# Two layers, two modulations: the second one's products and sums issued from the convolution's projection

## The chip, the core and the metric

The kernel is one program on one NeuronCore of a Trainium2 chip. TensorE multiplies matrices into PSUM (eight banks of 128 x 512 fp32), VectorE, ScalarE and GpSimd work beside it, and SyncE issues most of the loads. The engines run in parallel, each through its own list of instructions in order, and meet at semaphores. The metric is the time of one execution on the device, in microseconds, as the median of several runs.

## What is computed

A first block of two residual layers (sparse attention, then an RWKV mixer, each followed by a squared-ReLU feed-forward layer) and a second block of two conditioned layers (a short convolution, then dilated attention) on 256 tokens of 1024 features, all in fp32. What matters here is the conditioning of the second block:

```python
def adaln_pre_norm(x, c, g, w_mod, b_mod):
    mod = jax.nn.silu(c) @ w_mod + b_mod
    shift, scale, gate = jnp.split(mod, 3, axis=-1)
    h = rms_norm_2(x, g, NORM_EPS) * (1.0 + scale[:, None, :]) + shift[:, None, :]
    return h, gate

def short_conv_mixer(h, w_in, conv_k, w_out):
    b_gate, c_gate, xin, z = jnp.split(h @ w_in, 4, axis=-1)
    t = c_gate * xin
    ...
    return (b_gate * conv * jax.nn.silu(z)) @ w_out

# second block, i = 0 (convolution) and 1 (dilated attention)
    h, gate = adaln_pre_norm(x, c, norm_g[i], w_mod[i], b_mod[i])
    ...
    x = x + gate[:, None, :] * y
```

The modulation (shift, scale and gate) of both layers depends only on the condition `c` and the weights, so it can be worked out at any time before its use. That of layer 0 is used by the convolution, that of layer 1 by the dilated attention.

## The kernel before

The stages run one after the other: `dsa`, `mlp(0)`, `rwkv_in`, `rwkv_mid`, `scan_loop`, `rwkv_out`, `mlp(1)`, `mid_norm` (the first block's final norm, VectorE only), `conv`, `dilated`, `final_norm`. Each engine has a function of each of these names.

**Granules.** All large weights come in granules of 128 x 1024 fp32 (512 KB) through a ring of four slots (`RING = 4`). SyncE loads granule g into `raw`, ScalarE rounds it to `w_hi` (L585), VectorE takes the remainder `w_lo` (L1064), and TensorE multiplies it three times (hi by hi, lo by hi, hi by lo). ScalarE may round granule g once TensorE is done with granule g - 4. A block of the convolution's projection (`feature_granule`, L1765 to L1767) is four granules, 24 products each, into two banks. There are four blocks in each of two halves of the features: xin into banks 0 and 1, the gate c into 2 and 3, the gate b into 4 and 5, z into 6 and 7.

**Modulation.** During `mlp(l)` GpSimd loads the 24 pieces of `w_mod[l]` (L486), ScalarE scales them by the condition (L754) and GpSimd adds them up into `mod_all` (L492, L494). At the end of `mlp(l)`, after the last down product (L1950 to L1952), TensorE's `modulation(l)` sums `mod_all` over the partitions: 16 products of one column each give shift and scale in bank 7 (L1974), and two products of 512 columns give the gate in banks 6 and 0 (L1978). As fp32 each is two records in the profile, so 32 and 4. TensorE then waits until VectorE has taken them (`mod_ready`, four counts a layer): VectorE adds the bias (L1300), makes the gain (L1302) and adds both halves of the gate (L1307).

**The way into the convolution.** VectorE adds the down products to X (L1293), takes one more remainder (L1064), does its `modulation(1)`, and scales X in `mid_norm` (L1603) when GpSimd has the roots of the mean squares (L470, L472), which ScalarE's squares (L603) of the unscaled X feed. Then come the squares of the scaled X, their roots, the normalised rows (`normalise`, L1074), TensorE's transposes into banks 4 to 7 (L1789), gain and shift on VectorE (L1085), the rounding on ScalarE (L614), the remainder on VectorE (L1096) and the first product of the projection.

Of the kernel before, what the change touches and what calls it, by code (L numbers as in the profile page):

```python
# [8 lines left out]
F32R = mybir.dt.float32r  # L21
# [5 lines left out]
P = 128  # L27
SEQ = 256
TILES = SEQ // P
D = 1024  # L30
# [111 lines left out]
def program(nc, A, out):  # L142
    parts, _, parts_bf = shape_constants()
    with ExitStack() as keep:
# [101 lines left out]
        def mlp_plan(t):  # L246
            return dict(relu=t("ff_relu", [P, 2, BLOCK]), sq=t("ff_sq", [P, 2, BLOCK]),
                        mod_w=t("mod_w", [P, 3, D]),
                        mod_all=t("mod_all", [P, 3 * D]),
                        hi=t("ff_hi", [P, 2, 4, SEQ], F32R), lo=t("ff_lo", [P, 2, 4, SEQ], F32R))  # L250

# [807 lines left out]
        def _(dve):  # L1059
# [185 lines left out]
            def mlp(l, following):  # L1245
# [48 lines left out]
                split_lo(STREAM[following], PER_BLOCK - 1)  # L1294
                modulation(l)

            def modulation(l):

                dve.wait_ge(mod_full, 3 * l + 1)
                dve.tensor_tensor(mod_col[:, l, :], bank[7][:, 0:2 * KT], B_MOD[l], ALU.add).then_inc(mod_ready, 1)  # L1300
                dve.wait_ge(mod_ready, 4 * l + 1)
                dve.scalar_tensor_tensor(gain[:, l, :], mod_col[:, l, KT:2 * KT], 1.0, NORM2[l], ALU.add, ALU.mult).then_inc(mod_ready, 1)  # L1302
                dve.wait_ge(gate_loaded, 32)
                for n, b in enumerate((6, 0)):
                    dve.wait_ge(mod_full, 3 * l + 2 + n)
                    to = gate[:, l, n * BLOCK:(n + 1) * BLOCK]
                    dve.tensor_tensor(to, to, bank[b][:, :], ALU.add).then_inc(mod_ready, 1)  # L1307
# [297 lines left out]
            def conv():  # L1605
                base = STREAM["conv"]
                dve.wait_ge(x_updated, 18)
                normalise(5)
                dve.wait_ge(mod_ready, 8)
                scale_and_split(5, 4, gain[:, 0, :], mod_col[:, 0, 0:KT])  # L1610
# [8 lines left out]
                for half in range(2):  # L1619
                    at = 16 * half  # L1620
                    split_block(base, at + 4)
                    split_block(base, at + 8)

# [36 lines left out]
            def dilated():  # L1660
                base = STREAM["dil"]
                normalise(6)
                scale_and_split(6, 6, gain[:, 1, :], mod_col[:, 1, 0:KT])

# [73 lines left out]
        def _(pe):  # L1738
# [190 lines left out]
            def mlp(l):  # L1929
# [35 lines left out]
                down(FF_STEPS - 1, 4, 1, False, True)  # L1965
                modulation(l)

            def modulation(l):

                for n in range(3):  # L1970
                    pe.wait_ge(mod_used[n], KT * (l + 1))
                pe.wait_ge(up_relu, 2 * FF_STEPS * (l + 1))
                for k in range(2 * KT):
                    mm = pe.matmul(bank[7][:, k:k + 1], M["mod_all"][:, k * P:(k + 1) * P], ones[:, 0:1], start=True, stop=True)  # L1974
                mm.then_inc(mod_full, 1)
                for n, b in enumerate((6, 0)):
                    at = 2 * D + n * BLOCK
                    pe.matmul(bank[b][:, :], ones, M["mod_all"][:, at:at + BLOCK], start=True, stop=True).then_inc(mod_full, 1)  # L1978
                pe.wait_ge(mod_ready, 4 * (l + 1))

# [285 lines left out]
            def conv():  # L2266
# [3 lines left out]
                for half in range(2):  # L2270

                    for n, (left, count) in enumerate(((conv_x, 1), (conv_t, 1), (conv_b, 1), (conv_z, 2))):
                        if half:
                            pe.wait_ge(left, count)
                        for q in range(PER_BLOCK):
                            if n == half == 0:
                                wait_act(4, q)
                            g = base + 16 * half + 4 * n + q
                            feature_granule(g, g % RING, hi, lo, q, (bank[2 * n], bank[2 * n + 1]))
                pe.wait_ge(conv_x, 2)  # L2280
                pe.wait_ge(conv_t, 2)
# [106 lines left out]
```

## Time and profile before

| | us |
|---|---|
| median of 3 runs | 1340.64 |
| the runs | 1334.78 to 1341.19 |
| span of the profiled execution | 1330.5 |
| TensorE busy in it | 1210.7 |
| VectorE busy | 875.3 |
| ScalarE busy | 675.9 |
| GpSimd busy | 185.7 |

The span runs from the first to the last instruction; the runs' times also hold what lies around it. Times in rows are us from the span's start. The mean granted TensorE clock of the profiled execution is 0.954 of full speed. PE is TensorE, PEld its weight loads, DVE is VectorE, ACT ScalarE, POOL GpSimd. A row of a timeline gives the start, the time that its instructions cover, their line, what is written and read, how many there are, and in brackets how long the engine had no work before and who ended that.

### The profile page before, as it was taken

What the parts mean: (1) busy time and instruction counts of PE and PEld (TensorE: products, weight loads), DVE (VectorE), ACT (ScalarE), POOL (GpSimd) and SP (SyncE); (2) the same over time, 40 slices, a digit from 0 to 9 for tenths busy, and PEclk for the clock granted to TensorE, in tenths of its full rate; (3) what the DMA queues carried; (4) which work ended last, traced back from release to release, by engine and by line L of the source; (5) the groups of instructions that cost most, each with busy time, mean ns of one, the idle gap of its engine ahead of it and who ended that gap; (6) DMA issues with size and microseconds to landing.
All of it is one profiled execution on the core that took longest, in us unless ns stands there. A gap on an engine that the chain in (4) does not pass through costs nothing.

```text
span 1330.5 us, 21999 instructions
## 1 busy us (share of the span) xinstructions
PE 1210.7 (91%) x8300; PEld 1076.5 (81%) x8304; DVE 875.3 (66%) x1238; ACT 675.9 (51%) x1006; POOL 185.7 (14%) x168
## 2 busy tenths in 40 slices
PE   6889899999699789898989899998899799999986
PEld 5777798997598468887967889896899699998775
DVE  4785558687776566656436667777576777775674
ACT  4764465656254723333344556564443456665552
POOL 1000124345200010000000225253000000000000
PEclk9989999999899979899998999999899899999999
DMA  7321567876545100000003677776355645566300
GB/s 277 126 81 47 179 233 251 265 244 230 167 143 174 63 1 1 0 0 20 0 1 95 210 251 249 263 251 197 114 188 165 185 132 185 188 189 195 123 1 32
DMA packets 81882, 190.12 MB, mean 143 GB/s; under 512 B 5841, under 2 KB 6113, under 8 KB 81697
## 3 DMA queue, kind: packets, MB, share of 16 engines
q1 hardware_dynamic: 72896, 157.31, 36.5%
q0 software_dynamic: 7632, 27.59, 7.0%
q10 hardware_dynamic: 1296, 4.44, 0.9%
q8 instruction: 38, 0.62, 0.2%
q14 instruction: 20, 0.16, 0.0%
HBM read 188.27 MB, written 1.05 MB: 142 GB/s over the span
## 4 chain that ended last, share of the span: by engine, by line
PE 79%; DVE 10%; ACT 3%; issue 3%; POOL 2%; DMA 2%; ACTq 0%; DVEq 0%; POOLq 0%; SPq 0%
PE bank L1765 12%; PE bank L1767 12%; PE bank L1766 12%; PE bank L2080 7%; PE bank L1748 4%; PE bank L1750 4%; PE bank L1749 4%; PE bank L1950 4%; PE bank L1952 4%; PE bank L1951 4%; PE bank L2172 1%; POOL mod_all L494 1%; PE bank L1789 1%; PE bank L1991 1%; PE bank L2045 1%
## 5 line engine op out<-in xcount | busy, mean ns | idle before, releaser
L1064 DVE TENSOR_TENSOR w_lo<-raw,w_hi 128x1024 fp32r<-128x1024 f32 x296 | 390.8, 1336 | 248.6 <-ACT w_hi L585 248.5
L585 ACT ACTIVATE w_hi<-raw 128x1024 fp32r<-128x1024 f32 x296 | 311.8, 1058 | 348.5 <-PE bank L1767 176.7
L1765 PE MATMUL bank<-act_hi,w_hi 128*128 128x256 f32 x1392 | 391.9, 282 | 15.0 <-DMA rows_of<-in_rows_of_dram 9.4
L1767 PE MATMUL bank<-act_hi,w_lo 128*128 128x256 f32 x1392 | 390.8, 281 | 0.0
L1766 PE MATMUL bank<-act_lo,w_hi 128*128 128x256 f32 x1392 | 390.7, 281 | 0.0
L1765 PEld LDWEIGHTS bank<-act_hi,w_hi 128*128 128x128 f32 x1392 | 262.9, 189 | 17.3 <-DMA rows_of<-in_rows_of_dram 9.7
L1766 PEld LDWEIGHTS bank<-act_lo,w_hi 128*128 128x128 f32 x1392 | 262.9, 189 | 0.7 <-issue 0.2
L1767 PEld LDWEIGHTS bank<-act_hi,w_lo 128*128 128x128 f32 x1392 | 262.8, 189 | 0.0
L494 POOL TENSOR_TENSOR mod_all<-mod_all,mod_w 128x1024 f32<-128x1024 f32 x42 | 110.0, 2618 | 143.0 <-ACT mod_w L754 142.1
L1950 PE MATMUL bank<-w_hi,ff_hi 128*128 128x512 f32 x256 | 103.4, 404 | 5.9 <-DVE ff_lo L1262 5.9
L470 POOL TENSOR_SCALAR stat<-stat 128x1 f32<-128x1 f32 x16 | 9.0, 560 | 678.7 <-ACT xn L603 678.4
L1952 PE MATMUL bank<-w_hi,ff_lo 128*128 128x512 f32 x256 | 102.3, 400 | 0.0
L1951 PE MATMUL bank<-w_lo,ff_hi 128*128 128x512 f32 x256 | 101.6, 397 | 0.0
L1748 PE MATMUL bank<-w_hi,act_hi 128*128 128x512 f32 x224 | 89.8, 401 | 1.6 <-DVE act_lo L1585 1.2
L1750 PE MATMUL bank<-w_hi,act_lo 128*128 128x512 f32 x224 | 89.5, 400 | 0.0
L1749 PE MATMUL bank<-w_lo,act_hi 128*128 128x512 f32 x224 | 89.1, 398 | 0.0
L886 ACT ACTIVATE v_inv<-bank 128x512 f32<-128x512 f32 x56 | 33.4, 596 | 60.0 <-PE bank L2085 27.8
L1950 PEld LDWEIGHTS bank<-w_hi,ff_hi 128*128 128x128 f32 x256 | 48.9, 191 | 17.4 <-DVE w_lo L1064 6.7
L1952 PEld LDWEIGHTS bank<-w_hi,ff_lo 128*128 128x128 f32 x256 | 48.7, 190 | 12.6
L1951 PEld LDWEIGHTS bank<-w_lo,ff_hi 128*128 128x128 f32 x256 | 48.9, 191 | 11.1
L754 ACT ACTIVATE mod_w<-mod_w,c_col 128x1024 f32<-128x1024 f32 x48 | 51.7, 1137 | 6.0 <-DMA mod_w<-in_w_mod_dram 6.0
L1748 PEld LDWEIGHTS bank<-w_hi,act_hi 128*128 128x128 f32 x224 | 42.7, 190 | 13.7 <-DVE act_lo L1585 1.9
(285 smaller groups left out, 1734.0 us busy)
## 6 DMA issues: line engine op xcount, KB each, us to landing
raw<-in_mlp_w_up_dram SPq DMA_DIRECT2D x64, 512.0 KB, 4.9
raw<-in_mlp_w_down_dram SPq DMA_DIRECT2D x64, 512.0 KB, 4.3
raw<-in_dil_w_in_dram SPq DMA_DIRECT2D x64, 512.0 KB, 3.9
mod_w<-in_w_mod_dram POOLq DMA_DIRECT2D x48, 512.0 KB, 4.3
raw<-in_conv_w_in_dram SPq DMA_DIRECT2D x32, 512.0 KB, 3.6
raw<-in_rwkv_w_rkv_dram SPq DMA_DIRECT2D x24, 512.0 KB, 4.6
raw<-in_dsa_w_in_dram SPq DMA_DIRECT2D x16, 512.0 KB, 5.2
raw<-in_dsa_w_o_dram SPq DMA_DIRECT2D x8, 512.0 KB, 3.6
```

The source lines that it names most:

```text
L494: pool.tensor_tensor(total, total, part, ALU.add).then_inc(mod_used[n], 1)
L585: act.activation(w_hi[:, slot, :], raw[:, slot, :], ACT.Copy).then_inc(hi_ready, 1)
L1064: dve.tensor_tensor(w_lo[:, slot, :], raw[:, slot, :], w_hi[:, slot, :].bitcast(F32), ALU.subtract).then_inc(lo_ready, 1)
L1748: pe.matmul(dst, x_hi, w_hi[:, slot, at], start=begin, stop=False, skip_group_check=True)
L1749: pe.matmul(dst, x_hi, w_lo[:, slot, at], start=False, stop=False, skip_group_check=True)
L1750: mm = pe.matmul(dst, x_lo, w_hi[:, slot, at], start=False, stop=end, skip_group_check=True)
L1765: pe.matmul(dst, w_hi[:, slot, at], hi[:, kt, :], start=begin, stop=False, skip_group_check=True)
L1766: pe.matmul(dst, w_hi[:, slot, at], lo[:, kt, :], start=False, stop=False, skip_group_check=True)
L1767: mm = pe.matmul(dst, w_lo[:, slot, at], hi[:, kt, :], start=False, stop=end, skip_group_check=True)
L1950: pe.matmul(dst, x_hi, w_hi[:, at_slot, at], start=first and q == 0, stop=False, skip_group_check=True)
L1951: pe.matmul(dst, x_hi, w_lo[:, at_slot, at], start=False, stop=False, skip_group_check=True)
L1952: mm = pe.matmul(dst, x_lo, w_hi[:, at_slot, at], start=False, stop=last and q == PER_BLOCK - 1, skip_group_check=True)
```

## The change

The modulation of layer 1 is no longer issued at the end of `mlp(1)`, by neither TensorE nor VectorE; that of layer 0 stays at the end of `mlp(0)`.

- TensorE issues it in `conv`, after the first of the eight blocks of the projection. Its gate products go to banks 6 and 4, as bank 0 then holds the projection's xin.
- VectorE takes it in `conv` after the remainders of granules 4 to 7.
- TensorE waits for VectorE's part (`mod_ready`, 8) ahead of the third block, which writes bank 4, and no longer at the end of `mlp(1)`; for layer 0 that wait now stands in `mlp`.
- VectorE's wait for `mod_ready` in the convolution is for 4 instead of 8, and the dilated layer has one for 8.
- `mod_all` moves behind `ff_hi` and `ff_lo` in SBUF, so that the convolution's tiles don't lie over it.

```diff
         def mlp_plan(t):
             return dict(relu=t("ff_relu", [P, 2, BLOCK]), sq=t("ff_sq", [P, 2, BLOCK]),
                         mod_w=t("mod_w", [P, 3, D]),
-                        mod_all=t("mod_all", [P, 3 * D]),
-                        hi=t("ff_hi", [P, 2, 4, SEQ], F32R), lo=t("ff_lo", [P, 2, 4, SEQ], F32R))
+                        hi=t("ff_hi", [P, 2, 4, SEQ], F32R), lo=t("ff_lo", [P, 2, 4, SEQ], F32R),
+                        mod_all=t("mod_all", [P, 3 * D]))
...
                 split_lo(STREAM[following], PER_BLOCK - 1)
-                modulation(l)
+                if l == 0:
+                    modulation(l)
...
-                for n, b in enumerate((6, 0)):
+                for n, b in enumerate((6, 4 * l)):
                     dve.wait_ge(mod_full, 3 * l + 2 + n)
...
                 normalise(5)
-                dve.wait_ge(mod_ready, 8)
+                dve.wait_ge(mod_ready, 4)
                 scale_and_split(5, 4, gain[:, 0, :], mod_col[:, 0, 0:KT])
...
                     split_block(base, at + 4)
+                    if half == 0:
+                        modulation(1)
                     split_block(base, at + 8)
...
                 normalise(6)
+                dve.wait_ge(mod_ready, 8)
                 scale_and_split(6, 6, gain[:, 1, :], mod_col[:, 1, 0:KT])
...
                 down(FF_STEPS - 1, 4, 1, False, True)
-                modulation(l)
+                if l == 0:
+                    modulation(l)
+                    pe.wait_ge(mod_ready, 4)
...
-                for n, b in enumerate((6, 0)):
+                for n, b in enumerate((6, 4 * l)):
                     at = 2 * D + n * BLOCK
                     pe.matmul(bank[b][:, :], ones, M["mod_all"][:, at:at + BLOCK], start=True, stop=True).then_inc(mod_full, 1)
-                pe.wait_ge(mod_ready, 4 * (l + 1))
...
                         if half:
                             pe.wait_ge(left, count)
+                        elif n == 2:
+                            pe.wait_ge(mod_ready, 8)
                         for q in range(PER_BLOCK):
                             if n == half == 0:
                                 wait_act(4, q)
                             g = base + 16 * half + 4 * n + q
                             feature_granule(g, g % RING, hi, lo, q, (bank[2 * n], bank[2 * n + 1]))
+                        if n == half == 0:
+                            modulation(1)
```

## Rows read from the trace of the kernel before

**Rows 1.** The page: the chain by engine, and the costliest matmul group.
```profile
PE 79%; DVE 10%; ACT 3%; issue 3%; POOL 2%; DMA 2%; ACTq 0%; DVEq 0%; POOLq 0%; SPq 0%
...
L1765 PE MATMUL bank<-act_hi,w_hi 128*128 128x256 f32 x1392 | 391.9, 282 | 15.0 <-DMA rows_of<-in_rows_of_dram 9.4
```

**Rows 2.** Chain of waits, 924 to 941: start, duration, work or "issue".
```profile
924.63 3.46 PE bank L1974 x32
928.09 2.52 PE bank L1978 x4
...
934.07 0.56 POOL stat L472
...
934.73 0.76 DVE xn L1074
...
940.66 0.38 PE bank L1765
```

**Rows 3.** Timeline of VectorE, 921 to 945: start, duration, instruction, [idle before, releaser].
```profile
927.06 1.22 DVE L1064 TENSOR_TENSOR w_lo<-raw,w_hi 128x1024 fp32r<-128x1024 f32 x1
...
930.64 0.69 DVE L1307 TENSOR_TENSOR gate<-gate,bank 128x512 f32<-128x512 f32 x1 [0.79 <-PE bank L1978]
931.25 2.47 DVE L1603 SCALAR_TENSOR_TENSOR X<-X,stat,scale_row 128x1024 f32<-128x1024 f32 x2
```

**Rows 4.** Stretches by time: length; busy PE, PEld, DVE, ACT, POOL; TensorE clock; DMA.
```profile
912.10:915.30 3.20, 3.20 (x10) 2.42 (x9) 3.20 (x3) 1.15 (x2) 0.00 (x0) 0.50 0.76 224
924.60:928.80 4.20, 4.20 (x35) 3.82 (x34) 3.87 (x7) 3.36 (x5) 1.42 (x2) 1.00 0.43 126
929.50:939.00 9.50, 4.48 (x18) 3.28 (x16) 5.83 (x8) 2.30 (x4) 2.32 (x7) 0.50 0.32 107
941.00:1052.00 111.00, 111.00 (x859) 106.89 (x858) 70.74 (x90) 50.06 (x54) 0.00 (x0) 1.00 0.57 176
```

**Rows 5.** Waits: TensorE's (941 to 1052), then all engines' (951.9 to 1030).
```profile
PE bank L1765 <- DVE act_lo L1096: 1.4, 1, 1.4
...
ACT w_hi L585 <- PE bank L1767: 43.5, 26, 1.8
DVE w_lo L1064 <- ACT w_hi L585: 28.5, 21, 1.9
```

**Rows 6.** Timeline of TensorE at the transposes in front of the convolution.
```profile
935.63 3.01 PE L1789 MATMUL bank<-const,xn 128*128 128x128 f32 x13 [5.02 <-DVE xn L1074]
```

**Rows 7.** Timeline of GpSimd, 900 to 985.
```profile
927.30 1.03 POOL L470 TENSOR_SCALAR stat<-stat 128x1 f32<-128x1 f32 x1 [18.11 <-ACT xn L603]
928.41 0.58 POOL L472 TENSOR_TENSOR stat<-stat,half_neg 128x1 f32<-128x1 f32 x1
929.08 0.19 POOL L470 TENSOR_SCALAR stat<-stat 128x1 f32<-128x1 f32 x1
929.35 0.55 POOL L472 TENSOR_TENSOR stat<-stat,half_neg 128x1 f32<-128x1 f32 x1
```

**Rows 8.** Timeline of TensorE at the first layer's modulation, 343 to 351.
```profile
343.38 3.63 PE L1974 MATMUL bank<-const,mod_all 128*128 128x1 f32 x32
346.86 1.96 PE L1978 MATMUL bank<-mod_all,const 128*128 128x512 f32 x4
```

**Rows 9.** Stretches by time around the first layer's modulation, columns as in group 4.
```profile
362.10:365.50 3.40, 3.40 (x17) 3.40 (x18) 1.64 (x4) 0.63 (x1) 0.00 (x0) 0.50 0.00 0
366.30:369.70 3.40, 3.40 (x31) 3.40 (x30) 1.22 (x1) 1.07 (x2) 0.00 (x0) 1.00 0.00 0
343.40:350.20 6.80, 5.42 (x37) 4.12 (x35) 5.89 (x11) 3.36 (x5) 2.88 (x6) 1.00 0.49 162
```

**Rows 10.** Timeline of VectorE, 945 to 1090: the remainder of granule 7.
```profile
953.38 1.23 DVE L1064 TENSOR_TENSOR w_lo<-raw,w_hi 128x1024 fp32r<-128x1024 f32 x1 [1.59 <-ACT w_hi L585]
```

**Rows 11.** Stretches by time at the dilated layer's start, columns as in group 4.
```profile
1058.90:1062.00 3.10, 3.10 (x15) 3.10 (x16) 1.43 (x3) 0.00 (x0) 0.55 (x1) 0.50 0.47 153
1064.10:1067.50 3.40, 3.40 (x29) 3.40 (x30) 3.30 (x7) 1.55 (x3) 0.00 (x0) 1.00 0.00 0
```

## The prediction, made before the changed kernel was run

> **What bounds the kernel now.** I read the page first: TensorE stands for 79% of the chain that ended last, VectorE for 10% [rows 1]. So nearly everything waits for TensorE, but only averaged over stages; the change touches two, and each is read by itself.
>
> The first is the end of the second feed-forward layer. Its last product gives way at 924.63, and the chain of waits shows what follows until the convolution's first product at 940.66 [rows 2]: 3.46 us of one-column modulation products, 2.52 us of gate products, the last gate addition, the scaling of X from 931.25, its square on ScalarE, the root on GpSimd, the normalisation, the transposes, the modulated rows and their rounding. VectorE's timeline gives the same stretch from the other side [rows 3]: a weight remainder at 927.06, and at 930.64 the last gate addition after 0.79 us without work, ended by L1978. That addition stands straight in front of L1603.
>
> The second is the convolution's projection. The stretches by time show TensorE busy for all of 941 to 1052, at full clock [rows 4]. The lists of waits (951.9 to 1030) put ScalarE behind TensorE (43.5 us in 26 waits) and VectorE behind ScalarE (28.5 us in 21), and have no wait of TensorE in it [rows 5]. TensorE is the bound there and the others are paced by the ring of four granules.
>
> The change therefore takes TensorE work out of a place where TensorE then idles for 5.02 us [rows 6] and puts it into a place where it never idles.
>
> **Removed at the end of the feed-forward layer.** What is late next, once the modulation is gone? L1603 for the first row tile needs three things. VectorE is free of L1293 and its last w_lo at 927.06 + 1.22 = 928.28 [rows 3]. The bank sums in X are there. The root of the first tile ends on GpSimd at 928.41 + 0.58 = 928.99 [rows 7]. The root is the last, and L1074 starts 0.10 us after such a root (934.07 + 0.56 = 934.63, start 934.73) [rows 2]. So L1603 starts at 929.09 in place of 931.25: 2.16 us earlier. All that follows it up to 940.66 hangs on it in a chain [rows 2] and moves with it. Of the 5.98 us of TensorE work that leave, only these 2.16 us come back, as the path under them ran on VectorE, ScalarE and GpSimd anyway. Bounds: VectorE now runs L1603 while GpSimd works out the root of the second tile. L470 took 1.03 us beside a busy VectorE and 0.19 us alone [rows 7]; at the worst that root ends at 929.90 + 0.84 = 930.74, and the second L1603, due at 929.09 + 1.24 = 930.33, starts 0.5 us late. Gain 1.6 to 2.16 us; I take 2.16 because the second tile is ready at 929.90 if nothing interferes. The gate products also ran slower here (the clock was 1.00 up to 928.8 and 0.50 from 929.5 [rows 4]; 2.52 us against 1.96 us in the first layer [rows 2, 8]). Where it doesn't fall there, 0.6 us less is removed: lower bound 1.0 us.
>
> **Added to the projection.** After the first block (four granules, 96 products) TensorE runs the same 32 one-column records and four 512-column records. At full clock, in the first layer, they start at 343.38 and 346.86, so the first group takes 3.48 us; the second is busy for 1.96 us [rows 8], of which the next product would overlap about 0.17 us (a 256-column product lasts 0.28 us and they start 3.4/31 = 0.11 us apart [rows 1, 9]). Added: 3.48 + 1.96 - 0.17 = 5.27 us. TensorE idles nowhere in the projection, so all of it is on the path. Bounds 5.1 us (twice the overlap) and 5.98 us (3.46 + 2.52, half clock included [rows 2]).
>
> Does a later stall absorb it? In all of 941 to 1052 TensorE waits once, the 1.4 us in front of the first product [rows 5]. So nothing is given back, and the two terms sum to 5.27 - 2.16 = +3.11 us.
>
> **The moved waits.** VectorE takes its modulation after the remainders of granules 4 to 7 (the last of them starts at 953.38 and takes 1.23 us [rows 10], so it ends at 952.45 after the shift) and stands in front of granule 8. By the sum the first block (96 products at 3.4/29 = 0.117 us [rows 11], 11.2 us from 940.66 on) ends at 951.9 - 2.16 = 949.8, the last gate product at 955.0 and the last gate addition (0.69 us [rows 3]) ends at about 955.9. Granule 8's slot is free only when granule 4 is used, 2.8 us into the second block, at 957.9, and ScalarE's rounding comes first. Queued behind VectorE's wait are therefore only remainders that cannot start yet: cost nothing, margin over 2 us, and TensorE itself needs granule 8 only at 966. TensorE's new wait for the eighth modulation count stands at the third block, 11 us after the gate products: nothing. The removed wait at the end of the layer was over at 930.64 + 0.69 = 931.33 [rows 3], while TensorE waited for xn until 935.63 [rows 6]: nothing. VectorE's wait for count 4 in the convolution and for count 8 in the dilated layer have long been met: nothing. DMAs: none is moved. The weights' modulated sums are complete on GpSimd before 927.30 - 18.11 = 909.19, where its idle stretch begins [rows 7], and GpSimd's queue isn't passed by anything. The new place of mod_all only keeps the convolution's tiles off it.
>
> **The clock.** Two questions, both read from the granted clock. First, the products of the projection's start. TensorE will now stand idle from 924.6 to about 933.5 and then transpose. Before, the clock was 0.50 (1.2 GHz) from 929.5 to 939, transposes included, and 1.00 (2.4 GHz) from 941 [rows 4]. At the dilated layer's start the same happened: 0.50 under its transposes at 1058.9 to 1062, 1.00 from 1064.1 under its first products [rows 11]. In both, the projection behind the transposes ran at full clock, so I cost this at nothing.
>
> The Trainium skill (TensorE: Matmul & The Clock Gate, Part 4) says that in transpose mode the full clock isn't reached, as such work doesn't count as busy. By that rule the first products of the projection would run at half clock, as in the rival "cold start" below. The trace speaks against it in both places: 1.00 under the projection, after transposes that began at 0.50 [rows 4, 11].
>
> Second, the one-column products in mid-stream. In this layer they were followed by a fall to 0.50 between 928.8 and 929.5, with TensorE busy all the time from 924.6 [rows 2, 4]. In the first layer the clock was 1.00 over the products and after them (343.4 to 350.2) [rows 9]. So it can go either way. I take a fall, as the longer dense stretch behind them makes it dear and one of two shows it. A short slow stretch lasts from 912.1 to 915.3 [rows 4]. Its price comes from the products after 362: 17 in 3.4 us at half clock, 31 in 3.4 us at full clock [rows 9], that is 14 too few at 3.4/31 = 0.11 us, or 1.5 us (both counts take in products cut by the edges). Bounds: nothing, and two such stretches, 3.1 us.
>
> **Sum.** -2.16 + 5.27 + 1.5 = +4.6 us on the profiled execution, 1330.5 to 1335.1 us of span. The median of the runs, 1340.64, lies 10.1 us above that span, the lowest run, 1334.78, 4.3 us; I add the difference to the median: 1345.2 us, or +0.34%.
>
> **The rivals.**
> - *No fall of the clock in the projection* (speaks for it: the first layer): +3.11 us, 1343.8. Chance 0.22.
> - *Cold start*, by the longer idle stretch or because transposes don't raise the clock: they leave the clock at half and the projection's first 3.4 us run slow, on top of the fall behind the modulation: 3.11 + 1.5 + 1.5 = +6.1, 1346.8. Against it: the two places above. Chance 0.10. The Trainium skill's rule would end here.
> - *Slower by more than can be missed*: the one-column products hold the clock down over two stretches. This is one mechanism, from 950 on in the projection, where weight loads fill TensorE but each product is one column. It is 3.11 + 3.1 = +6.2 with the gain at its full size, and with the gain at its lower bound of 1.0 us +7.4, 1348.0. It decides against the kernel from two slow stretches on. Chance 0.18.
> - *The moved products cost nothing*, as TensorE isn't what paces the projection: -2.16, 1338.5. For it: ScalarE and VectorE each work only half of the time and could catch up. Against: they wait for TensorE, not it for them [rows 5]. Chance 0.05.
> - *The removal gives nothing*, as GpSimd's roots are as late as the gate was: 5.27 + 1.5 = +6.8, 1347.4. Against: 928.99 and 929.90 [rows 7]. Chance 0.03.
> - The forecast has the rest, 0.42.
>
> **How the numbers follow.** About 0.5% (6.7 us) is what a measurement of this kernel can tell from no change; the three runs shown already differ by 6.4 us. Faster by more than that (below 1333.9) comes out of no case but the spread of the runs: 0.03. Slower by more (above 1347.3) takes the slower rival, half of the removal that gives nothing, and a part of cold start: 0.20. The rest is 0.77. The range goes from the case in which the products are free (1338.5), a little lower for the spread of the runs, to the slower rival: 1337.5 to 1349.
>
> **What the profile after should show.** L1603 starts about 4.5 us after the last down product (6.6 us before). TensorE idles about 9 us in front of its transposes, in place of 5.0. The 36 modulation records stand between the convolution's first and second block with no idle time before or behind them and take 5.3 us. From the last down product to the end of the convolution's last block the time grows by 3 to 5 us, and behind that everything is shifted alike. If VectorE's w_lo for granule 8 comes later than 1.5 us after its slot is free, the step on the moved wait is wrong. If the stretch behind the modulation has a clock of 1.00, the clock term is wrong. If TensorE shows an idle stretch in the projection before or after, so is the claim that it is the bound.

## The result: 0.5% slower, and the profile after

The changed kernel took 1344.38 us (median of 10 runs, 1339.68 to 1345.73) against 1337.55 us for the kernel before (10 runs, 1330.52 to 1341.39). The ratio is 1.005 with a 95% interval of 1.0030 to 1.0069: 6.7 us slower, between 4.0 and 9.2. The forecast was +4.6 us, 1345.2 us; it stood on the first three runs of the kernel before, whose median was 3.1 us above that of the ten.

The page of the changed kernel (span, then the chain that ended last by engine):

```profile
span 1341.1 us, 22000 instructions
...
PE 79%; DVE 10%; ACT 3%; issue 3%; POOL 2%; DMA 2%; ACTq 0%; DVEq 0%; POOLq 0%; SPq 0%
```

The shares are those of [rows 1]. The difference is in two stages, so they are read like the stages before. First the end of the feed-forward layer. VectorE's timeline of the changed kernel, against [rows 3]:

```profile
927.24 2.48 DVE L1281 TENSOR_TENSOR X<-X,bank 128x512 f32<-128x512 f32 x4 [0.42 <-PE bank L1944]
929.63 1.22 DVE L1052 TENSOR_TENSOR w_lo<-raw,w_hi 128x1024 fp32r<-128x1024 f32 x1
931.66 1.29 DVE L1592 SCALAR_TENSOR_TENSOR X<-X,stat,scale_row 128x1024 f32<-128x1024 f32 x1 [0.81 <-POOL stat L460]
933.39 1.28 DVE L1592 SCALAR_TENSOR_TENSOR X<-X,stat,scale_row 128x1024 f32<-128x1024 f32 x1 [0.44 <-POOL stat L460]
935.47 0.75 DVE L1062 TENSOR_SCALAR xn<-X,stat 128x1024 f32<-128x1024 f32 x1 [0.79 <-POOL stat L460]
```

The last down product was done when VectorE started its additions at 927.24; L1592, the old L1603, starts 4.42 us later (before: 931.25 - 924.66 = 6.59). It is released by L460, GpSimd's root, as the sum said. But its second half waits 0.44 us for the other root. GpSimd's timeline, against [rows 7]:

```profile
931.90 1.45 POOL L460 TENSOR_TENSOR stat<-stat,half_neg 128x1 f32<-128x1 f32 x1
...
934.22 0.51 POOL L458 TENSOR_SCALAR stat<-stat 128x1 f32<-128x1 f32 x1 [0.77 <-ACT xn L591]
```

The second L460 takes 1.45 us beside VectorE's L1592; in the kernel before it took 0.55 [rows 7]. At 934.22 the next L458 takes 0.51 us beside the second L1592, which now lies later; in the kernel before, the same root's first half, at 933.79, took 0.19 us with VectorE idle. TensorE's timeline, against [rows 2, 6] in front of the projection and against [rows 8] for the moved products:

```profile
936.28 3.67 PE L1781 MATMUL bank<-const,xn 128*128 128x128 f32 x16 [9.08 <-DVE xn L1062]
941.33 0.58 PE L1757 MATMUL bank<-act_hi,w_hi 128*128 128x256 f32 x1 [1.38 <-DVE act_lo L1084]
```

```profile
954.81 3.63 PE L1968 MATMUL bank<-const,mod_all 128*128 128x1 f32 x32
958.30 2.63 PE L1972 MATMUL bank<-mod_all,const 128*128 128x512 f32 x4
959.95 1.20 PE L1757 MATMUL bank<-act_hi,w_hi 128*128 128x256 f32 x1
```

TensorE is idle for 9.08 us in place of 5.02, and the first product comes at 941.33. The 36 records stand in the projection with no idle time before or behind. Its stretches by time (columns as in [rows 4]):

```profile
932.60:941.30 8.70, 3.67 (x16) 3.27 (x16) 5.66 (x10) 3.52 (x6) 2.78 (x7) 0.50 0.31 101
941.40:945.50 4.10, 4.10 (x19) 4.10 (x20) 3.58 (x7) 1.26 (x2) 0.00 (x0) 0.50 0.00 0
946.10:954.70 8.60, 8.60 (x75) 8.60 (x74) 3.68 (x3) 3.18 (x3) 0.00 (x0) 1.00 0.39 120
954.80:959.30 4.50, 4.50 (x37) 4.02 (x36) 1.57 (x3) 2.03 (x3) 0.00 (x0) 1.00 0.56 157
959.60:962.60 3.00, 3.00 (x11) 2.21 (x10) 1.29 (x2) 0.00 (x0) 0.00 (x0) 0.50 0.25 96
963.10:1034.00 70.90, 70.90 (x600) 70.90 (x599) 41.06 (x51) 30.68 (x32) 0.00 (x0) 1.00 0.56 172
```

The projection now has two slow stretches that it had not in the kernel before: its first 4 us (941.4 to 945.5), and 959.6 to 962.6 behind the one-column products. TensorE is busy in all of them.

### The profile page after: what moved, and what is told of

It is laid out like the page before. It is cut to its first block, busy times and chain, and to the rows that moved or that the text cites. A ratio compares the mean times of both kernels' runs of the same rounds, so it can differ in the third digit from the quotient of the medians.

```text
span 1341.1 us, 22000 instructions
## 1 busy us (share of the span) xinstructions
PE 1218.2 (91%) x8300; PEld 1083.5 (81%) x8304; DVE 875.8 (65%) x1238; ACT 676.3 (50%) x1006; POOL 186.8 (14%) x168
## 4 chain that ended last, share of the span: by engine, by line
PE 79%; DVE 10%; ACT 3%; issue 3%; POOL 2%; DMA 2%; ACTq 0%; DVEq 0%; POOLq 0%; SPq 0%
PE bank L1757 12%; PE bank L1758 12%; PE bank L1759 12%; PE bank L2073 7%; PE bank L1740 4%; PE bank L1742 4%; PE bank L1741 4%; PE bank L1942 4%; PE bank L1944 4%; PE bank L1943 4%; PE bank L2165 1%; POOL mod_all L482 1%; PE bank L1984 1%; PE bank L1781 1%; PE bank L2038 1%
## 5 line engine op out<-in xcount | busy, mean ns | idle before, releaser
L1757 PE MATMUL bank<-act_hi,w_hi 128*128 128x256 f32 x1392 | 395.9, 284 | 13.7 <-DMA rows_of<-in_rows_of_dram 8.3
L1757 PEld LDWEIGHTS bank<-act_hi,w_hi 128*128 128x128 f32 x1392 | 266.1, 191 | 16.6 <-DMA rows_of<-in_rows_of_dram 8.7
L1758 PEld LDWEIGHTS bank<-act_lo,w_hi 128*128 128x128 f32 x1392 | 266.0, 191 | 1.3 <-issue 0.8
L1759 PEld LDWEIGHTS bank<-act_hi,w_lo 128*128 128x128 f32 x1392 | 265.8, 191 | 0.0
L458 POOL TENSOR_SCALAR stat<-stat 128x1 f32<-128x1 f32 x16 | 9.1, 568 | 685.6 <-ACT xn L591 685.2
```

The source lines that it names most:

```text
L1757: pe.matmul(dst, w_hi[:, slot, at], hi[:, kt, :], start=begin, stop=False, skip_group_check=True)
L1758: pe.matmul(dst, w_hi[:, slot, at], lo[:, kt, :], start=False, stop=False, skip_group_check=True)
L1759: mm = pe.matmul(dst, w_lo[:, slot, at], hi[:, kt, :], start=False, stop=end, skip_group_check=True)
```

## The experiments

Runs of one and the same kernel differ by up to 15 us here (35 runs of the kernel before: 1329.68 to 1344.45), so a comparison of whole times tells 2 to 3 us apart at best. The traces tell more. I read the same three marks in every trace: VectorE's first addition of the down products into X (a), the first product of the convolution's projection (b), and the first product of its output layer (c). "Way in" is a to b, "projection" b to c. All kernels have the same 768 products between b and c; "pace" is their mean distance where they stand close. "Cold" tells whether the clock was 0.50 under the projection's first products, "fall" whether it was 0.50 right behind the products of the modulation.

| kernel | way in, us | projection, us | pace, us | cold | fall | time against before (95%) |
|---|---|---|---|---|---|---|
| before | 16.00 | 90.22 | 0.1173 | no | | |
| before_again | 16.26 | 90.21 | 0.1173 | no | | 0.9995 (0.9976 to 1.0014) |
| changed | 14.09 | 100.10 | 0.1187 | yes | yes | 1.0050 (1.0030 to 1.0069) |
| after_again | 14.10 | 97.05 | 0.1173 | from about 1 us on | no | 1.0056 (1.0031 to 1.0082) |
| after_third | 14.10 | 98.84 | 0.1174 | yes | yes | 1.0062 (1.0043 to 1.0081) |
| no_mod | 14.10 | 90.22 | 0.1173 | no | | 0.9998 (0.9976 to 1.0021) |
| add_only | 15.95 | 97.28 | 0.1175 | no | yes | 1.0059 (1.0038 to 1.0080) |
| cols_only | 14.15 | 96.22 | 0.1185 | no | yes | 1.0032 (1.0014 to 1.0051) |
| gates_only | 14.19 | 94.79 | 0.1185 | yes | no | 1.0020 (1.0002 to 1.0037) |
| spread | 14.11 | 97.68 | 0.1174 | yes | no | 1.0030 (1.0009 to 1.0050) |
| after_warm | 13.61 | 97.12 | 0.1173 | no | yes | 1.0047 (1.0027 to 1.0067) |
| pe_early | 13.82 | 91.22 | 0.1187 | no | | 0.9989 (0.9966 to 1.0012) |
| lora_late | 13.69 | 91.89 | 0.1173 | yes | | 0.9960 (0.9940 to 0.9981) |
| best_warm | 14.31 | 91.72 | 0.1173 | yes | | 0.9956 (0.9938 to 0.9975) |

**The kernels themselves again.** No edit.

> The kernel before against itself: what such a comparison can tell from no change, and a second trace. Ratio 1.000. From the last down product to the projection's first product 16.0 us, the projection 90.2 us at a pace of 0.1173 us and 91.2 at 0.1187; if the projection starts at half clock here too, up to 2 us more, and then the cold start isn't the removal's doing.

> The changed kernel once more, for a second trace and for the spread. Main theory (2.2 us come back at the end of the feed-forward layer, 5.3 us are added to the projection, and the clock falls once behind the moved products for 1.5 us): +4.6 us. Cold start in addition (the projection's first products at half clock for about 4.6 us, as in the first trace of the changed kernel, +2.2 us): +6.8 us. The trace shows which: under cold start the granted clock is 0.50 again under the projection's first products. Rival 'pace' (in the first trace of the changed kernel the products of the whole convolution stood 0.1187 us apart, not 0.1173 as before, +1 us over the projection): the pace is 0.1187 again in every trace of this program.

> The changed kernel a third time. Two questions: does the clock fall behind the moved one-column products (it did in one of two traces of this kernel, and in the traces of the two experiments that move or repeat those products in one piece), and does the projection start at half clock (it did in the first trace; in the second the clock fell 1 us after the start). With both: 90.2 + 5.3 + 1.5 + 1.7 to 2.0 = 98.9 us at the faster pace; with neither 95.5.

The kernel before against itself gives 0.9995. Its way in is 16.26 us, 0.26 more than in the first trace, so differences of the way in against the kernel before are known to 0.3 us only. The changed kernel's way in is 14.10 us in all three traces. Its projection is 100.10, 97.05 and 98.84. The last was expected at 98.9 from the four terms, and came out at 98.84. "Pace" as a property of the program fell: the same program ran at 0.1187 in one trace and 0.1173 and 0.1174 in the others. It isn't one of the execution either: in the first trace of the kernel before, the products stand 0.1173 us apart in the convolution and 0.1187 in the dilated layer (1100 to 1140). The second trace shows that both clock terms can come otherwise:

```profile
942.80:943.50 0.70, 0.70 (x6) 0.70 (x7) 0.70 (x3) 0.00 (x0) 0.00 (x0) 1.00 0.00 0
944.10:947.00 2.90, 2.90 (x16) 2.90 (x15) 2.27 (x5) 0.77 (x2) 0.00 (x0) 0.50 0.00 0
947.60:955.40 7.80, 7.80 (x69) 7.80 (x69) 3.68 (x3) 3.01 (x3) 0.00 (x0) 1.00 0.42 128
955.60:960.40 4.80, 4.80 (x37) 4.17 (x36) 1.64 (x4) 2.03 (x3) 0.00 (x0) 1.00 0.58 167
```

It starts at full clock, falls for one stretch from 944.1, and stays at 1.00 under and behind the one-column products (955.6 to 960.4). So all three traces show a slow stretch near the projection's start, and two of three one behind the products.

**The removal alone.** The dilated layer then takes layer 0's gain and shift, and its gate is the bias alone.

```diff
                     split_block(base, at + 4)
-                    if half == 0:
-                        modulation(1)
...
-                        if n == half == 0:
-                            modulation(1)
```

> The changed kernel without layer 1's modulation on TensorE and VectorE (the dilated layer takes layer 0's gain and shift, and its gate is the bias alone). It has the removal and nothing of the addition. Main theory: -2.2 us against the kernel before, and 6.8 us less than the changed kernel. If the cold start belongs to the removal (TensorE idle for 9 us ahead of the transposes): -2.2 + 2.2 = 0 us and the clock at 0.50 under the projection's first products. If the addition costs nothing: the same as the changed kernel.

The way in is 14.10 us like the changed kernel's, 1.9 us under before and 2.2 under before_again, and the projection is 90.22 us, before's figure to the last digit. The whole time, 0.9998, can't tell -2 us from nothing. So this gain is shown by the traces only.

**The addition alone.** Against the changed kernel (VectorE's part too is back at the end of the layer, and nobody takes the second set of results):

```diff
                 split_lo(STREAM[following], PER_BLOCK - 1)
-                if l == 0:
-                    modulation(l)
+                modulation(l)
...
-                if l == 0:
-                    modulation(l)
-                    pe.wait_ge(mod_ready, 4)
+                modulation(l)
+                pe.wait_ge(mod_ready, 4 * (l + 1))
...
                         if n == half == 0:
-                            modulation(1)
+                            modulation(1, (6, 4))
```

> The other half: layer 1's modulation stays at the end of the feed-forward layer on both engines as before, and TensorE issues its 18 products a second time behind the projection's first block, where nobody reads them. Main theory: +5.3 for the products and +1.5 for the fall of the clock, +6.8 us against before. Without a fall: +5.3. If TensorE isn't the bound of the projection: 0. No cold start is expected beyond what the kernel before has, as TensorE is busy at the layer's end as before.

The products and the stretch behind them, in TensorE's timeline and in the stretches by time:

```profile
951.79 3.63 PE L1964 MATMUL bank<-const,mod_all 128*128 128x1 f32 x32
955.28 2.95 PE L1968 MATMUL bank<-mod_all,const 128*128 128x512 f32 x4
```

```profile
940.40:951.60 11.20, 11.20 (x95) 11.20 (x96) 7.22 (x10) 4.45 (x5) 0.00 (x0) 1.00 0.30 92
956.40:959.40 3.00, 3.00 (x10) 1.97 (x9) 0.00 (x0) 0.00 (x0) 0.00 (x0) 0.50 0.29 111
```

The projection grew by 97.28 - 90.22 = 7.06 us, of which 5.3 are the products, 0.2 the pace (768 x 0.0002) and the rest, 1.6 us, the slow stretch from 956.4. The time, 1.0059, is that of the changed kernel. "TensorE isn't the bound" would have given 90.2.

**Which part makes the clock fall.** The two kinds of products one by one, and then both as in the change but the one-column products in four groups:

```diff
 # cols_only: gate products stay at the end of the layer
+                else:
+                    gates(l)
+                    pe.wait_ge(mod_ready, 6)
...
                         if n == half == 0:
-                            modulation(1)
+                            columns(1)
```

> Only the 16 one-column products (and VectorE's shift and gain) move into the projection, at the place of the change; the two gate products and both gate additions stay at the end of the feed-forward layer. In the trace: 3.5 us in the projection, and behind them the clock falls for one stretch of 3.4 us at 0.50, which costs 1.5 us, if the fall belongs to the one-column products: the projection takes 90.2 + 5.0 = 95.2 us. If the fall belongs to anything that interrupts the projection, the same; if it is chance, 93.7. From the last down product to the first product of the projection about 14.7 us, against 16.0 before, as VectorE's gate additions end at about 5 us after it. Total against before: about +3.7 us, in time hard to tell from no change.

```diff
 # gates_only: one-column products stay at the end of the layer
+                else:
+                    columns(l)
+                    pe.wait_ge(mod_ready, 6)
...
                         if n == half == 0:
-                            modulation(1)
+                            gates(1, (6, 4))
```

> Only the two gate products (and both gate additions) move into the projection; the one-column products, shift and gain stay at the end of the layer. In the trace: 1.8 us in the projection and no fall of the clock behind them, 92.0 us for the projection, if the fall belongs to the one-column products; 93.5 if it belongs to any interruption. From the last down product to the first product of the projection 14.1 us like the changed kernel, as nothing of the modulation then stands between VectorE's weight remainder and GpSimd's root. Total: -1.9 + 1.8 = 0 us.

```diff
 # spread
                             feature_granule(g, g % RING, hi, lo, q, (bank[2 * n], bank[2 * n + 1]))
+                            if n == half == 0:
+                                columns(1, range(4 * q, 4 * q + 4), 3)
                         if n == half == 0:
-                            modulation(1)
+                            gates(1, (6, 4))
+                            pe.wait_ge(mod_ready, 6)
```

> The changed kernel with its 16 one-column products in four groups of four, one behind each granule of the projection's first block (into bank 3), and the gate products behind the block as before. The same instructions in the same stage, so the same 5.3 us. If the fall of the clock comes from one-column products standing together, the granted clock stays at 1.00 behind them and the projection takes 90.2 + 5.3 = 95.5 us; if it comes with them wherever they stand, 97.0 as in the second trace of the changed kernel. Total: -1.9 + 5.3 = +3.4 us against before.

The stretches by time around the products, of cols_only, gates_only and spread in this order:

```profile
956.50:959.40 2.90, 2.90 (x15) 2.90 (x15) 0.31 (x2) 0.00 (x0) 0.00 (x0) 0.50 0.54 179
```

```profile
940.80:944.80 4.00, 4.00 (x19) 4.00 (x20) 3.58 (x7) 1.26 (x2) 0.00 (x0) 0.50 0.00 0
945.80:954.00 8.20, 8.20 (x72) 8.20 (x72) 3.67 (x3) 3.18 (x3) 0.00 (x0) 1.00 0.41 130
954.10:956.00 1.90, 1.90 (x8) 0.94 (x7) 0.58 (x1) 1.67 (x3) 0.00 (x0) 1.00 0.54 165
956.00:1034.00 78.00, 78.00 (x660) 78.00 (x659) 48.74 (x65) 33.37 (x35) 0.00 (x0) 1.00 0.53 172
```

```profile
943.50:947.20 3.70, 3.70 (x17) 3.70 (x18) 3.60 (x7) 1.26 (x2) 0.00 (x0) 0.50 0.00 0
948.00:962.20 14.20, 14.06 (x112) 12.75 (x110) 5.21 (x7) 5.21 (x6) 0.00 (x0) 1.00 0.34 112
```

Behind the one-column products in one piece the clock is 0.50; behind the gate products, and behind the same one-column products in four groups (948 to 962.2 holds them all), it is 1.00. The two expectations for the projection were still missed, 95.2 and 92.0 against 96.22 and 94.79 measured, and for the spread products 95.5 against 97.68. The terms that were not in them close the first two: the pace of 0.1185 adds 768 x 0.0012 = 0.9 us to each (95.2 + 0.9 = 96.1), and gates_only starts cold (940.8 to 944.8), 1.8 us (92.0 + 0.9 + 1.8 = 94.7). Spread starts cold too (95.5 + 1.8 = 97.3); 0.4 us stay open there, perhaps the four changes between kinds of products (not shown). Two more expectations were missed: the way in of cols_only, 14.15 us against 14.7 (VectorE's gate additions were over at 932.09, 4.8 us after the mark, and X followed at once), and the time of gates_only, expected unchanged and found at 1.0020 (1.0002 to 1.0037), with the cold start and the pace. The whole time of spread, 1.0030, lies below the changed kernel's, but the intervals overlap.

So in one piece the one-column products were followed by a fall in five traces of six (changed, after_third, add_only, cols_only, after_warm; not after_again), and in other arrangements in none of two.

That a fall is not certain is shown better by the first layer, whose modulation no version moves. All 14 traces have the same 32 records there, at 343 to 349 us. In six of them (before_again, changed, after_again, gates_only, pe_early, best_warm) the clock falls 4.5 to 4.9 us after the first of these products, in the eight others not within 11.8 us. The stretches by time of changed (products from 343.61) and of after_third (from 342.96):

```profile
348.50:355.20 6.70, 4.66 (x18) 3.28 (x16) 4.48 (x8) 0.00 (x0) 5.38 (x8) 0.50 0.50 141
```

```profile
343.00:354.90 11.90, 7.44 (x53) 5.82 (x51) 10.33 (x19) 3.99 (x6) 7.76 (x12) 1.00 0.50 146
```

What goes with it in this place is when the products begin: 8.77 to 9.12 us after the last slow stretch ended in the six traces with a fall, 8.20 to 8.65 us in the eight without. In the projection the changed kernel's three traces fit too (9.0 and 9.3 us with a fall; 8.4 without, in after_again). At the end of the second layer they don't all: with 8.6 us in gates_only and 8.1 in pe_early the clock fell. So the fall often comes with these products, and with their place in time as well; the one trace of spread without a fall can be chance, and that spreading the products prevents it is not shown.

**The cold start.** TensorE is kept busy with useless products in its idle stretch:

```diff
                 if l == 0:
                     modulation(l)
                     pe.wait_ge(mod_ready, 4)
+                else:
+                    pe.wait_ge(up_relu, 2 * FF_STEPS * (l + 1))
+                    for f in range(34):
+                        pe.matmul(bank[0][:, :], hi[:, 0, 0:P], hi[:, 0:2, :].rearrange("p k t -> p (k t)"), start=True, stop=True)
```

```profile
927.50:935.30 7.80, 7.61 (x34) 5.95 (x32) 6.09 (x7) 4.91 (x8) 4.15 (x8) 1.00 0.43 134
936.00:941.00 5.00, 2.19 (x16) 1.72 (x16) 3.68 (x8) 1.26 (x3) 0.87 (x2) 1.00 0.27 99
941.10:952.20 11.10, 11.10 (x95) 11.10 (x96) 7.24 (x10) 4.45 (x5) 0.00 (x0) 1.00 0.29 92
957.00:960.00 3.00, 3.00 (x10) 1.97 (x9) 1.38 (x2) 0.00 (x0) 0.00 (x0) 0.50 0.27 105
```

The clock is 1.00 through the transposes (936 to 941) and the first products, the way in is 13.61 us (13.6 was expected), and the fall behind the moved products at 957 is there as before. The two marks together are 110.73 us against 112.94 in after_third, 2.2 us less, with equal pace; of the whole time the ratios 1.0047 and 1.0062 agree with that but their intervals overlap. With TensorE idle for 5.7 to 9.1 us ahead of the transposes (changed, after_again, after_third, spread, gates_only, no_mod, cols_only) five traces of seven have the slow stretch at the start. Where the whole modulation or filling products stood there (idle for 5.0 us at most) it is two of seven (lora_late and best_warm have it; before, before_again, add_only, after_warm and pe_early don't). That the longer idle stretch makes the cold start more frequent is possible by these counts, but not shown: seven traces a side are few. The dilated layer, where no version changes the work at the start and TensorE is idle for 5.4 us in all 14 traces, has a slow start in six (changed, after_again, before_again, no_mod, gates_only, pe_early). A slow start behind an idle stretch is thus common here without any edit, and after_warm's one trace could be of the kind that starts fast anyway.

**A version that keeps the gain.** TensorE issues the products at the end of the layer, gate halves into banks 0 and 1, and VectorE takes the gate halves later:

```diff
+                gate_half(1, 0)
                 normalise(5)
-                dve.wait_ge(mod_ready, 4)
+                gate_half(1, 1)
                 scale_and_split(5, 4, gain[:, 0, :], mod_col[:, 0, 0:KT])
...
+                pe.wait_ge(mod_ready, 5)
                 turn(5, xn, 4 * TILES)
+                pe.wait_ge(mod_ready, 8)
```

> A version that takes the gain without the price: TensorE issues layer 1's products where it idles anyway, at the end of the feed-forward layer (gate halves into banks 0 and 1), and VectorE takes the columns there, but the two gate halves only behind the scaling of X and behind the normalisation, in its idle stretches of 0.8 to 1.1 us. Main theory: -2.2 us against before, like the kernel without the modulation, and 6.8 us less than the changed kernel. If what costs 2.2 us in the kernel before is not VectorE's wait for the gate products: 0.

Both gate additions on VectorE's timeline of pe_early:

```profile
931.10 0.17 DVE L1291 TENSOR_TENSOR mod_col<-bank,pcol 128x16 f32<-128x16 f32 x1 [1.13 <-PE bank L1975]
931.31 0.17 DVE L1293 SCALAR_TENSOR_TENSOR gain<-mod_col,pcol 128x8 f32<-128x8 f32 x1
931.40 2.48 DVE L1600 SCALAR_TENSOR_TENSOR X<-X,stat,scale_row 128x1024 f32<-128x1024 f32 x2
933.92 0.69 DVE L1299 TENSOR_TENSOR gate<-gate,bank 128x512 f32<-128x512 f32 x1
934.82 0.76 DVE L1062 TENSOR_SCALAR xn<-X,stat 128x1024 f32<-128x1024 f32 x1 [0.22 <-POOL stat L460]
...
936.96 0.68 DVE L1299 TENSOR_TENSOR gate<-gate,bank 128x512 f32<-128x512 f32 x1
937.57 1.90 DVE L1073 TENSOR_SCALAR act_f<-bank,gain,mod_col 128x256 f32<-128x256 f32 x4
```

The way in is 13.82 us, 2.2 less than before, although the clock fell under the one-column products in this trace (they ended late, and L1600 waited for the gain: it started 5.05 us after the mark, not 4.42). The time, 0.9989, is 0.7% under 1.0056, the changed kernel's on the same chip, and can't be told from before's.

The trace of the kernel before also shows TensorE idle for 9.4 us in front of the first RWKV product, until a load (rows_of) that this product doesn't read [rows 1]. So pe_early with one wait moved:

```diff
-                pe.wait_ge(lora_loaded, 16 * 6)
...
                     if n == 3:
+                        pe.wait_ge(lora_loaded, 16 * 6)
                         lora(0, ((0, LORA),))
```

> The version with TensorE's early products and VectorE's late gate additions, and in addition TensorE's wait for the small RWKV weights moved from the front of that stage to their first use. The trace of the kernel before shows TensorE idle for 9.4 us there with that load named as the releaser. Theory: the first mixed rows are ready 5 us or more before the load, so 5 to 6 us come back: -7 to -8 us against before. Rival: the wait hides another one, on the mixed rows' remainders or on the ring, and less than 2 us come back.

```profile
350.30 2.02 PE L1788 MATMUL bank<-const,xn 128*128 128x128 f32 x16 [1.61 <-DVE xn L1062]
355.74 0.58 PE L1764 MATMUL bank<-act_hi,w_hi 128*128 128x256 f32 x1 [3.42 <-DVE act_lo L1323]
```

TensorE now waits 3.42 us, for VectorE's remainder: 6.0 of the 9.4 us came back at this place, as the theory said. The rest was another wait underneath. The time is 0.9960 (0.9940 to 0.9981), about 5 us under before: this version beats both kernels. Expected were 7 to 8 us; the interval, 2.5 to 8.0 us, just reaches that, its middle doesn't. Why is open.

> The fastest kernel so far (TensorE's products early, VectorE's gate additions late, the wait for the small RWKV weights at their first use) with 16 useless products behind the modulation, 3.7 us, to keep TensorE busy until shortly before the transposes. If a busy TensorE keeps the clock up: 0.5 us less in front of the projection and no cold start in it, 1 to 2 us faster than without, -6 to -7 us against before. If not: like that kernel, -5 us.

That gave 0.9956, no more than without. The filling products were mis-sized: the clock had fallen under the modulation, they took 5.45 us and not 3.7, and the transposes started 1.3 us late (10.4 us after the mark, 9.1 in lora_late). The cold start was there all the same.

## Why the prediction was right

By its own steps, with the figure forecast and the figure found:

- **What comes back at the end of the layer: 2.16, found 1.9 to 2.2** (14.10 against 16.00 and 16.26). The first L1603 moved by 6.59 - 4.42 = 2.17 us, to 0.01 us of the step. The bound named beside it ("VectorE now runs L1603 while GpSimd works out the root") came true: L460 1.45 us, L458 0.51. Against the first trace that took 0.25 us. It should have been in the sum, as the step had found the cause.
- **What is added: 5.27, found 5.2 to 5.3.** In add_only the one-column group takes 3.49 us from start to start (951.79 to 955.28). In gates_only the gate products start at 954.07 and the second product behind them at 955.90, so they take 955.90 - 0.12 - 954.07 = 1.7 us at full clock. All of it is on the path; the whole projection still has no wait of TensorE.
- **The moved waits: nothing, found nothing.** In the changed kernel the last gate addition ends at 960.97 + 0.69 = 961.66, and ScalarE rounds granule 8 only at 964.79:

```profile
955.07 1.06 ACT L573 ACTIVATE w_hi<-raw 128x1024 fp32r<-128x1024 f32 x1 [1.78 <-PE bank L1759]
...
964.79 1.06 ACT L573 ACTIVATE w_hi<-raw 128x1024 fp32r<-128x1024 f32 x1 [7.69 <-PE bank L1759]
```

```profile
ACT w_hi L573 <- PE bank L1759: 49.4, 25, 7.7
DVE w_lo L1052 <- ACT w_hi L573: 30.3, 20, 4.2
```

ScalarE's one long wait, 7.7 us, is for TensorE, so the ring still follows TensorE as in [rows 5]. VectorE was free 4.2 us before it was needed.

- **The fall of the clock: 1.5, found 1.5 to 1.6 where it occurs**, in five traces of six. The choice against "no fall" was right, but it stood on one row of two, and in the first layer, from which the other row came, it is six traces of fourteen. That it came out is in part luck.
- **The cold start: nothing, with a chance of 0.10. This is the term that failed.** The changed kernel has a slow stretch at the start of the projection in all three of its traces, at 1.5 to 2.0 us each. Two places in one trace had been taken for a rule. The same stage's counterpart, the dilated layer's start, shows how little they bear: it was at full clock under its first products in the kernel before and cold at 1074.67 in the changed kernel's first trace, with no edit near it. The counts would have priced it at 0.8 us (six traces of fourteen, at the dilated layer) to 1.2 us (five of seven, after a long idle stretch).
- **From the span to the median: not understood.** The prediction left open why the median lay 10.1 us above the span. The changed kernel's profiled execution took 1342.85 us for a span of 1341.1, so 1.7 us lie around the span, and the profile of before was one of its fast executions (1330.5 + 1.7 = 1332.2, an estimate). It did no harm, as the difference was added to the median. But that median, 1340.64, was itself 3.1 us above the 1337.55 of ten runs. That 1345.2 stands only 0.8 us from the measured 1344.38 is luck: the difference was forecast 2.1 us too small.

With the changed kernel's own cold starts (1.5 to 2.0 us, in three traces of three) the sum is -1.9 + 5.3 + 1.5 x 2/3 + 1.75 = +6.2 us; the marks of the traces give (112.76 - 106.35) = +6.4 us (means of three and two traces, way in and projection together), and the time +6.7 (4.0 to 9.2). All three are nearer to the rival "cold start" (+6.1, chance 0.10) than to the forecast, and its mechanism, a cold start and a fall behind the products, is what two of the three traces show. Of the other rivals, "costs nothing" and "the removal gives nothing" fell by add_only and no_mod. "Slower by more than can be missed" was right about the size in the first trace (+8.0 us between the outer marks) for another reason: two slow stretches, but one before and one behind the products, and 1 us of pace.

The Trainium skill's rule (TensorE: Matmul & The Clock Gate, Part 4) on transposes is not borne out as it stands: in the traces of before, before_again, after_again, no_mod, cols_only and add_only the clock rose from 0.50 to 1.00 with nothing but transposes since the idle stretch, ahead of the first product. The stretches by time of no_mod, whose first product starts at 946.94:

```profile
938.40:944.60 6.20, 2.72 (x13) 2.73 (x14) 3.16 (x5) 2.30 (x4) 2.58 (x7) 0.50 0.41 138
945.20:946.90 1.70, 0.07 (x1) 0.00 (x0) 1.70 (x5) 1.21 (x2) 0.00 (x0) 1.00 0.00 0
```

## What to carry to other kernels

Work that stands in the bottleneck engine's idle stretch costs there only what the chain really waits for it (here about 2 us of 6), and only that comes back when it leaves. Moved into a stretch where that engine never waits, it costs its full length (here 5.3 us). What to move is the other engine's half: issue the products early, and let VectorE take the results where its own timeline has gaps.

A TensorE stage that starts behind an idle stretch should have a slow start in the sum at its frequency over several traces, not at what one trace happened to show; and a change of 5 us in a kernel whose runs differ by 15 is read from marks in several traces.

## What the runs showed of the hardware

- The same program's fp32 products of 256 columns stood 0.1173 us apart in the convolution in some executions and 0.1187 in others (0.1185 in two), 1.2% apart with the granted clock at 1.00 in both; two stages of one execution can differ in the same way. What sets it was not found.
- The spread of the runs goes with the mean granted clock: the 35 runs of the kernel before that stood beside after_again go from 1329.68 us at a mean clock of 0.956 to 1344.45 us at 0.947.
- Sixteen one-column products in one piece (3.5 us with weight loads back to back) were followed by a fall to 1.2 GHz in five traces of six in the projection and in six of fourteen at the end of the first layer, although TensorE shows as busy up to the fall; the same products in four groups were not, in one trace.
- GpSimd's one-column L460 (L472 in the kernel before) took 0.55 us with VectorE idle (934.07), 0.55 us beside VectorE's gate addition out of PSUM (929.35), and 1.45 us beside its L1592, which scales X in SBUF.
- With no edit near it, the dilated layer's first products ran in part at 1.2 GHz in six traces of fourteen, behind the same 5.4 us of idle TensorE.
